# Two attention stages with the value matmuls moved ahead of one head's transposes

## The chip, the cores and the metric

The kernel runs on one core of a Trainium2 chip. The metric is the device time of one launch in microseconds (us); lower is better. TensorE is written PE, VectorE DVE, ScalarE ACT, GpSimd POOL and SyncE SP.

## The reference

Two transformer blocks follow each other on a sequence of 1024 tokens with 1024 channels, all in float32. The change touches the attention of each. The first block has neighbourhood attention with 8 heads of 64 channels: a token sees 8 rows by 16 columns of a grid of 16 by 64 tokens. The second has full attention with 8 query heads that share 2 key and value heads:

```
def attend_block(q_blk):
    scores = jnp.einsum('bqhgd,bkhd->bhgqk', q_blk, k).astype(jnp.float32) * scale
    p = jax.nn.softmax(scores, axis=-1).astype(v.dtype)
    return jnp.einsum('bhgqk,bkhd->bqhgd', p, v)
```

Around them lie the input projections, a chunked delta-rule recurrence, a Fourier mixer, output projections and two SwiGLU networks. None of those is touched.

## The kernel before

Every engine has its own program, written out as a Python loop of instructions and semaphore waits, and each engine does its program strictly in order. The phases follow each other: input projection, neighbourhood attention ("na"), delta rule, output projection, first SwiGLU, mixer, full attention ("gqa"), output projection, second SwiGLU. Both attention phases are made by the same functions (`pe_attention`, `act_attention`, `dve_attention`, `pool_attention`).

The work of an attention phase is 32 pairs. A pair is two heads (j = 0 and 1, side by side in the partitions) by 128 query tokens; pairs 8c to 8c+7 belong to the c-th couple of heads. In gqa a pair has 1024 keys. In na it has 512 keys in four of eight pairs (t = 0, 1, 6, 7) and 576 in the other four. PE's loop has n + 4 = 36 steps. In step i, as far as the pairs exist, it does:

- the scores of pair i, both heads, into two PSUM slots of two banks each (`sring`); line 820. It waits until the slots are free: in gqa until ACT has taken the exponentials of both heads of pair i - 1, in na until DVE has added the bias and found the maxima.
- the transposes of head 1 of pair i - 1, 128 keys each, up to four to a PSUM bank; line 836. They wait for that head's exponentials.
- half of the value matmuls of two pairs, i - 3 or thereabouts: `values((i - 3) // 2, (i - 3) % 2)`; line 856. Part 0, in odd steps, waits until both heads of pair i - 2 have been copied out of PSUM.
- once in four steps, from step 5 on, `spread`: four instructions at line 865 that turn the sums of four pairs into a row of factors in one PSUM bank.
- the transposes of head 0 of pair i - 1.
- in gqa, `aside(i)`: pieces of the norm and rotation of the next couple's queries, with matmuls of their own at line 2149 (steps 1, 9, 17) and line 2156 (steps 5, 13, 21). They write into `sring` too.

Transposes and `spread` take their banks from one ring of three (`tring`). A bank is free once its content has been copied: that of head 1 by DVE (line 974), that of head 0 by ACT (line 341), the `spread` bank by ACT (line 341, the scale copy). With 1024 or 576 keys a head takes two banks, with 512 keys one; below, "a" and "b" are a head's first and second bank.

ACT's step i: exponentials of pair i, head 0, then head 1 (line 918, each with a read of the accumulated sum behind it); the scale copy if there is one; the copies of head 0 of pair i - 1; its asides. DVE's step i: the maxima of pair i, head 0, then head 1 (line 968 in gqa, 963 and 346 in na); once in four steps a reciprocal; the copies of head 1 of pair i - 1; once in four steps, the product with the scales (line 993), and its asides.

Of the kernel before, what the change touches and what calls it, by code (L numbers as in the profile page):

```python
# [111 lines left out]
def build(nc, A):  # L112
# [673 lines left out]
    def value_steps(u):  # L786
        if u.nk % 128 == 0:
            return [(i, 128, 0, 256) for i in range(u.nk // 128)]
        return [(1, 128, 0, 256), (2, 128, 0, 256), (3, 128, 0, 256), (0, 128, 0, 128), (4, 64, 0, 128),
                (4, 128, 128, 256), (5, 64, 128, 256)]  # L790

    def group_at(S, i, after):

        g = (i - after - 3) // 4
        if i >= after + 3 and (i - after - 3) % 4 == 0 and g < len(S.pairs) // 4:
            return g

    def pe_attention(e, w, S, operands, aside):

        T, pairs = S.T, S.pairs
        n = len(pairs)

        def scores(u):
            (qh, ql), (kh, kl), _, ready = operands(u)
            places = [S.sring.take((u.i, j), [(S.top if S.bias else S.exp, (u.i, j))]) for j in range(2)]
            for _, before in places:
                for s, key in before:
                    w.wait_ge(s, key)  # L810
            for s, key in ready:
                w.wait_ge(s, key)
            a = tok[u.t]
            for c in u.banks:
                b = slice(c, min(u.nk, c + 512))
                k = slice(u.k0 + b.start, u.k0 + b.stop)
                for x, (q, kk) in enumerate(((qh, kh), (qh, kl), (ql, kh))):
                    for j in range(2):
                        r = rows_of(j)
                        m = e.matmul(places[j][0][:, b], q[r, a], kk[r, k], start=x == 0, stop=x == 2)  # L820
                        if x == 2 and c == u.banks[-1]:
                            m.then_inc(*S.score.up((u.i, j)))

        def turn_bank(key, until):
            p, before = S.tring.take(key, until)
            for s, key in before:
                w.wait_ge(s, key)
            return p

        def transposes(u, j):  # L830
            w.wait_ge(S.exp, (u.i, j))
            for c0 in u.banks:
                p = turn_bank((u.i, c0, j), [(S.copied[j], (u.i, c0))])
                for c in range(c0, min(u.nk, c0 + 512), 128):
                    k = min(128, u.nk - c)
                    m = e.transpose(p[0:k, c - c0:c - c0 + 128], S.P(u.i, j)[:, c:c + k], IDENT)  # L836
                m.then_inc(*S.turn.up((u.i, c0, j)))

        def values(two, part):
            u = pairs[2 * two + 1]  # L840
            _, _, V, ready = operands(u)
            steps = value_steps(u)
            if part == 0:
                if two >= 2 and two % 2 == 0:
                    w.wait_ge(S.out, two // 2 - 1)
                for s, key in ready:
                    w.wait_ge(s, key)
                for j in range(2):
                    w.wait_ge(S.copied[j], u.last)
            q0 = 256 * (two % 2)  # L850
            half = (len(steps) + 1) // 2
            for x in (range(half), range(half, len(steps)))[part]:
                kt, k, a, b = steps[x]
                v = u.base // 128 + kt
                for j in range(2):
                    m = e.matmul(S.o[rows_of(j), q0 + a:q0 + b], V[0:k, v, rows_of(j)], S.PT(u.i, j)[0:k, kt, a:b],  # L856
                                 start=x == 0, stop=x == len(steps) - 1)
            m.then_inc(*S.value.up((two, part)))

        def spread(g):  # L860

            p = turn_bank(("scale", g), [(S.scale, g)])
            w.wait_ge(S.diag, g)
            for j in range(2):
                m = e.matmul(p[rows_of(j), :], ONES[:, 0:64], T.diag[:, j, :, :].rearrange("p t n -> p (t n)"),
                             start=True, stop=True)
            m.then_inc(*S.spread.up(g))

        for i in range(n + 4):
            if i < n:  # L870
                scores(pairs[i])
            if 0 <= i - 1 < n:
                transposes(pairs[i - 1], 1)
            if 0 <= i - 3 < n:
                values((i - 3) // 2, (i - 3) % 2)
            g = group_at(S, i, 2)
            if g is not None:
                spread(g)
            if 0 <= i - 1 < n:
                transposes(pairs[i - 1], 0)  # L880
            aside(i)

# [145 lines left out]
    def pe_na(e, w):  # L1028
        pe_attention(e, w, NA, na_operands, lambda i: None)
# [1206 lines left out]
    def pe_gqa(e, w):  # L2236
        def values():
            p = gq_place(w, "v", [(v_copy, 0)])
            w.wait_ge(first_load[1], 1)
            for t in tok:  # L2240
                m = e.transpose(p[:, t], Q_.first[1][:, t], IDENT)
            m.then_inc(*v_turn.up(0))
        first_norms(e, w, pe_norm, values)
        pe_attention(e, w, GQ, gqa_operands, norms_between(e, w, pe_norm))
# [382 lines left out]
```

## Time and profile before

| | |
|---|---|
| median of the runs shown (3001.87 to 3010.09) | 3004.83 us |
| the profiled execution | 3002.75 us |
| its span in the trace | 3001.0 us |
| PE busy | 2738.3 us, 91% of the span |
| ACT, DVE, POOL busy | 37%, 40%, 40% |
| na attention on PE, first scores to last full step | 466.8 to about 582 us |
| gqa attention on PE, its end | about 2173 us |

The span runs from the first to the last instruction; the profiled execution's own time is 1.75 us longer, and is the one that compares with the runs. The maxima, exponentials and copies of both attention phases run beside PE on their own engines. A matmul's record begins when PE starts it, and its end is modelled, so the distance from one start to the next is what PE spends; a transpose's record is 0.27 us long although one starts every 0.11 us.

### The profile page before, as it was taken

The numbers are of one execution on the slowest core, as the hardware profiler recorded it, in microseconds if no ns is written. First come the engines' busy times: TensorE is split into PE (matmuls) and PEld (weight loads), VectorE is DVE, ScalarE is ACT, GpSimd is POOL, SyncE is SP. The second block draws the span as 40 slices with busy tenths as digits, with TensorE's granted clock in tenths as the row PEclk, the third lists the DMA queues.
The fourth block names the chain that finished last, engine by engine and source line by source line (L and its number), as shares of the span: only waits on it lengthen the run. The fifth ranks groups of instructions, "written<-read, shape, count | busy, mean of one in ns | idle before, by whom it ended". The sixth has DMA issues, their size and how long they took to land.

```text
span 3001.0 us, 33532 instructions
## 1 busy us (share of the span) xinstructions
PE 2738.3 (91%) x13547; PEld 2196.6 (73%) x13547; DVE 1185.7 (40%) x1729; ACT 1097.1 (37%) x1604; POOL 1187.6 (40%) x568
## 2 busy tenths in 40 slices
PE   6999987936969999999999999479999999999997
PEld 4777774536968888878888788356678888788885
DVE  6565555576574222222222421367652221222223
ACT  4444435513443422233322422256544222332222
POOL 2212112230006545556555643311165555565554
PEclk8999998968989999999999999799999999999998
DMA  3223203262034222232222232200032222233322
GB/s 125 88 95 127 91 39 121 80 227 67 24 101 146 97 99 98 92 105 99 98 99 99 97 127 78 85 8 8 2 126 98 99 98 93 98 107 104 114 98 77
DMA packets 96330, 280.05 MB, mean 93 GB/s; under 512 B 26344, under 2 KB 26536, under 8 KB 96048
## 3 DMA queue, kind: packets, MB, share of 16 engines
q1 hardware_dynamic: 96176, 277.91, 26.8%
q8 instruction: 108, 1.77, 0.2%
q14 instruction: 46, 0.38, 0.0%
HBM read 245.30 MB, written 32.57 MB: 93 GB/s over the span
## 4 chain that ended last, share of the span: by engine, by line
PE 80%; DVE 8%; ACT 4%; DMA 2%; issue 2%; POOL 2%; SPq 1%; POOLq 0%; DVEq 0%; ACTq 0%
PE ps L325 22%; PE ps L326 22%; PE ps L327 22%; ACT t L341 3%; PE ps L820 3%; PE ps L836 2%; PE ps L856 2%; PE ps L466 1%; DVE t L1288 1%; DVE t L1285 1%; DVE t L600 1%; DVE t L968 1%; POOL t L1660 1%; DVE t L963 1%; POOL t L390 0%
## 5 line engine op out<-in xcount | busy, mean ns | idle before, releaser
L341 ACT ACTIVATE t<-t 128x1024 fp32r<-128x1024 f32 (+5 forms) x981 | 751.3, 810 | 1578.1 <-PE ps L327 677.2
L390 POOL TENSOR_TENSOR t<-t 128x1024 fp32r<-128x1024 f32 x363 | 875.9, 2416 | 1001.0 <-ACT t L341 1001.0
L325 PE MATMUL ps<-t 128*128 128x512 f32 (+1 forms) x3096 | 1223.0, 395 | 50.9 <-DVE t L503 19.0
L326 PE MATMUL ps<-t 128*128 128x512 f32 (+1 forms) x3096 | 1207.1, 390 | 0.0
L327 PE MATMUL ps<-t 128*128 128x512 f32 (+1 forms) x3096 | 1206.9, 390 | 0.0
L325 PEld LDWEIGHTS ps<-t 128*128 128x128 f32 x3096 | 584.5, 189 | 191.9 <-issue 55.3
L326 PEld LDWEIGHTS ps<-t 128*128 128x128 f32 x3096 | 584.9, 189 | 122.3 <-issue 5.4
L327 PEld LDWEIGHTS ps<-t 128*128 128x128 f32 x3096 | 584.6, 189 | 121.6
L1876 DVE SCALAR_TENSOR_TENSOR t<-ps,t 128x512 f32<-128x512 f32 x192 | 132.7, 691 | 315.7 <-PE ps L327 277.2
L1932 POOL TENSOR_TENSOR t<-t 128x512 fp32r<-128x512 f32 x84 | 108.8, 1296 | 332.3 <-ACT t L341 332.3
L1853 DVE TENSOR_TENSOR t<-ps,t 128x512 f32<-128x512 f32 x84 | 58.1, 692 | 396.2 <-PE ps L327 396.2
L1847 DVE TENSOR_TENSOR t<-ps,t 128x512 f32<-128x512 f32 x88 | 60.9, 692 | 329.8 <-PE ps L327 329.7
L341 ACT ACTIVATE t<-ps 128x512 f32<-128x512 f32 (+5 forms) x230 | 116.1, 541 | 123.7 <-PE ps L1208 37.5
L820 PE MATMUL ps<-t 64*128 64x512 f32 (+1 forms) x672 | 91.9, 402 | 46.0 <-POOL t L1048 22.2
L836 PEld LDWEIGHTS ps<-t 128*128 128x128 f32 (+1 forms) x800 | 85.5, 140 | 58.8 <-issue 25.5
L836 PE MATMUL ps<-t 128*128 128x128 f32 (+1 forms) x800 | 119.1, 283 | 9.5 <-DVE t L974 9.4
L942 POOL TENSOR_TENSOR t<-t 128x1024 f32<-128x1024 f32 x16 | 30.6, 1911 | 232.7 <-DVE t L985 206.8
L820 PEld LDWEIGHTS ps<-t 64*128 64x128 f32 x672 | 61.3, 192 | 69.9 <-issue 49.1
L918 ACT ACTIVATE t<-ps,t 128x1024 f32<-128x1024 f32 x64 | 71.4, 1115 | 95.7 <-DVE t L968 95.5
L856 PE MATMUL ps<-t 128*64 128x256 f32 (+2 forms) x864 | 102.8, 372 | 1.4 <-ACT t L341 1.4
L968 DVE TENSOR_REDUCE t<-ps 128x1 f32<-128x1024 f32 x64 | 75.3, 1218 | 52.0 <-PE ps L820 52.0
L1660 POOL TENSOR_TENSOR t<-t 128x512 f32<-128x512 f32 x56 | 79.8, 1426 | 25.7 <-ACT t L341 25.7
(148 smaller groups left out, 1872.3 us busy)
## 6 DMA issues: line engine op xcount, KB each, us to landing
t<-in_wts_dram SPq DMA_DIRECT2D x363, 512.0 KB, 3.5
t<-pj SPq DMA_DIRECT2D x42, 512.0 KB, 5.6
pj<-t SPq DMA_DIRECT2D x32, 512.0 KB, 3.2
t<-in_rpb_dram SPq DMA_DIRECT2D x8, 736.0 KB, 6.3
t<-in_xT_dram SPq DMA_DIRECT2D x8, 512.0 KB, 10.9
t<-grow_d SPq DMA_DIRECT2D x8, 512.0 KB, 6.3
t<-beta_d SPq DMA_DIRECT2D x8, 512.0 KB, 6.7
t<-in_xT_dram SPq DMA_DIRECT2D x16, 256.0 KB, 3.8
```

The lines of the kernel that those rows point to most:

```text
L325: e.matmul(out, ah, bh, start=start, stop=False)
L326: e.matmul(out, ah, bl, start=False, stop=False)
L327: return e.matmul(out, al, bh, start=False, stop=stop)
L341: return e.activation(out, in_, fn, scale=scale)
L390: e.tensor_tensor(lo[:], T.raw[n % NR][:], hi[:].bitcast(F), SUB).then_inc(*w_lo.up(n))
L820: m = e.matmul(places[j][0][:, b], q[r, a], kk[r, k], start=x == 0, stop=x == 2)
L836: m = e.transpose(p[0:k, c - c0:c - c0 + 128], S.P(u.i, j)[:, c:c + k], IDENT)
L856: m = e.matmul(S.o[rows_of(j), q0 + a:q0 + b], V[0:k, v, rows_of(j)], S.PT(u.i, j)[0:k, kt, a:b], start=x == 0, stop=x == len(steps) - 1)
L968: e.tensor_reduce(nmx[:, 0:1], p, AX, MAX, negate=True).then_inc(*S.neg.up((u.i, j)))
L1660: e.tensor_tensor(acc, acc, squares, ADD).then_inc(*b_acc.up((stage, s, k)))
L1876: e.scalar_tensor_tensor(X[:, o, h], banks[P.name, s, i, o], 0.5, X[:, o, h], MUL, ADD).then_inc(*P.x_ready(s, i, o)[0].up((P.name, s, i, o)))
L1932: e.tensor_tensor(al, P.up(j), ah.bitcast(F), SUB).then_inc(*f_lo.up((P.name, j)))
```

## The change

The transposes of head 1 move from before the value matmuls to directly before those of head 0. No instruction is added or removed, and the other engines' programs stay as they are. `tring` hands out its banks in the order of PE's program, so the bank of `spread` now comes before those of head 1.

```diff
         for i in range(n + 4):
             if i < n:
                 scores(pairs[i])
-            if 0 <= i - 1 < n:
-                transposes(pairs[i - 1], 1)
             if 0 <= i - 3 < n:
                 values((i - 3) // 2, (i - 3) % 2)
             g = group_at(S, i, 2)
             if g is not None:
                 spread(g)
             if 0 <= i - 1 < n:
+                transposes(pairs[i - 1], 1)
                 transposes(pairs[i - 1], 0)
             aside(i)
```

## Rows read from the trace of the kernel before

**Rows 1.** The page, section 1: busy us, share of the span, instructions.

```profile
PE 2738.3 (91%) x13547; PEld 2196.6 (73%) x13547; DVE 1185.7 (40%) x1729; ACT 1097.1 (37%) x1604; POOL 1187.6 (40%) x568
```

**Rows 2.** Windows: length, busy us by engine, PEclk, DMA share, GB/s.

```profile
480.00:582.00 102.00, 99.70 (x793) 62.64 (x790) 67.68 (x211) 68.69 (x158) 34.50 (x16) 1.00 0.20 73
1976.00:2173.00 197.00, 181.16 (x1362) 119.80 (x1360) 129.60 (x149) 113.19 (x196) 29.46 (x14) 1.00 0.02 6
2013.00:2024.00 11.00, 7.75 (x50) 4.60 (x50) 4.78 (x5) 4.94 (x8) 0.00 (x0) 1.00 0.00 0
```

**Rows 3.** Timeline, gqa, step 16: start us, duration us, instructions, idle before.

```profile
2062.19 1.66 PE L820 MATMUL ps<-t 64*128 64x512 f32 x12
...
2063.79 1.09 PE L836 MATMUL ps<-t 128*128 128x128 f32 x8
2063.89 2.35 DVE L968 TENSOR_REDUCE t<-ps 128x1 f32<-128x1024 f32 x2 [1.97 <-PE ps L820]
...
2064.81 1.95 PE L856 MATMUL ps<-t 128*64 128x256 f32 x16
...
2066.27 1.24 DVE L974 COPY t<-ps 128x512 f32<-128x512 f32 x2
2066.28 1.12 ACT L918 ACTIVATE t<-ps,t 128x1024 f32<-128x1024 f32 x1
...
2066.69 1.09 PE L836 MATMUL ps<-t 128*128 128x128 f32 x8
2067.29 0.19 ACT L918 ACTIVATION_READ_ACCUMULATOR t<-ps,t 128x1 f32 x1
...
2067.71 0.50 PE L820 MATMUL ps<-t 64*128 64x512 f32 x2
```

**Rows 4.** Timeline, gqa, PE in step 32, which has no scores.

```profile
2163.27 2.00 PE L836 MATMUL ps<-t 128*128 128x128 f32 x16
```

**Rows 5.** Timeline, gqa, end of step 12, where DVE is late.

```profile
2039.39 1.24 DVE L974 COPY t<-ps 128x512 f32<-128x512 f32 x2
...
2040.08 0.66 PE L836 MATMUL ps<-t 128*128 128x128 f32 x4 [0.79 <-DVE t L974]
2040.41 0.19 ACT L918 ACTIVATION_READ_ACCUMULATOR t<-ps,t 128x1 f32 x1
...
2040.75 0.51 PE L820 MATMUL ps<-t 64*128 64x512 f32 x2
```

**Rows 6.** Timeline, gqa, step 17: with spread and the matmul of line 2149.

```profile
2070.33 1.95 PE L856 MATMUL ps<-t 128*64 128x256 f32 x16
...
2071.80 1.11 ACT L918 ACTIVATE t<-ps,t 128x1024 f32<-128x1024 f32 x1
...
2072.11 1.03 PE L865 MATMUL ps<-t 128*64 128x512 f32 x4
...
2073.07 1.09 PE L836 MATMUL ps<-t 128*128 128x128 f32 x8
2073.18 1.66 ACT L341 ACTIVATE t<-ps 128x512 f32<-128x512 f32 x3 [0.18 <-PE ps L865]
...
2075.93 1.96 PE L2149 MATMUL ps<-t 128*128 128x512 f32 x4 [1.77 <-ACT t L341]
```

**Rows 7.** Timeline, gqa, step 21: with spread and the matmul of line 2156.

```profile
2102.41 1.12 ACT L918 ACTIVATE t<-ps,t 128x1024 f32<-128x1024 f32 x1
...
2104.12 1.88 PE L2156 MATMUL ps<-t 128*128 128x512 f32 x4
```

**Rows 8.** Timeline, na, from step 25, which has spread.

```profile
562.26 0.97 PE L820 MATMUL ps<-t 64*128 64x512 f32 x6
...
562.62 0.58 ACT L341 ACTIVATE t<-ps 128x512 f32<-128x512 f32 x1
...
563.75 1.08 PE L856 MATMUL ps<-t 128*64 128x256 f32 x8
```

**Rows 9.** Timeline, na, PE's first scores after a long idle.

```profile
466.84 1.65 PE L820 MATMUL ps<-t 64*128 64x512 f32 x6 [22.24 <-POOL t L1048]
```

## The prediction

> **What bounds the kernel now.** I read the page first: PE is busy 91% of the span and no other engine above 40% [rows 1]. The change touches only the two attention phases, so I then took windows of them. In na PE is busy 99.70 of 102 us; in gqa 181.16 of 197 us; the granted clock is 1.00 in both, the 2.4 GHz level [rows 2]. So the change plays in about 320 us, of which PE idles some 20. Last I read the timeline step by step, since what matters is what follows what.
>
> A plain gqa step is 5.52 us from scores to scores (2062.19 to 2067.71) [rows 3]. PE has no gap in it: scores take 1.60 to the next start, head 1's transposes 1.02, values 1.88, head 0's transposes 1.02. But a second chain is nearly as long. The scores start 2062.19; DVE's maxima start 2063.89 and end 2066.24; ACT's second exponential starts 2066.28, and its read of the sum ends 2067.29 + 0.19 = 2067.48; only then is the slot free for the next scores, at 2067.71. How long PE needs from such a release is seen where PE did wait: the read ended 2040.41 + 0.19 = 2040.60 and the scores started 2040.75, so 0.15 [rows 5]. The chain alone therefore allows 2067.63: 5.44 us a step. **PE is only 0.08 us above the chain of scores, maxima and exponentials.** That is the reader's key to gqa: shortening PE's part gives 0.08 us a step at most.
>
> **What the change saves on PE.** Two things. First, two runs of eight transposes become one of sixteen. Step 32 has one: 2.00 us, against 1.02 + 1.09 = 2.11 for two separate ones [rows 3, 4]: 0.11 saved. Second, scores are followed by values in place of transposes. Before transposes PE spends more than before matmuls: values take 1.88 to the next start when transposes follow (2064.81 to 2066.69) and 1.78 when `spread` follows (2070.33 to 2072.11) [rows 3, 6]. No row has values behind scores. I take the bounds as 0.10 saved (the full difference just read) and 0.10 lost (the same size the other way, as nothing here excludes it), and choose 0.10 saved, since values and `spread` have the same stationary shape. Together 0.21 us a step, between 0.21 and 0.01.
>
> **Plain gqa steps.** Does the new order find its banks free? Count from the scores' start as 0. Values at 1.50, head 1's transposes at 1.50 + 1.88 = 3.38, their first bank ready at 3.38 + 0.66 = 4.04. DVE leaves its maxima at 2066.27, which is 4.08, so it loses nothing. Its copy takes about 0.64 to 0.68 (1.24 to 1.28 for two), to 4.74. Head 0's second bank is the one just copied (four banks a step from a ring of three); a waiting transpose started 0.05 behind such a copy (2039.39 + 0.64 = 2040.03, then 2040.08) [rows 5]. So it may start at 4.79; unhindered it would at 3.38 + 12/16 of 1.93 = 4.83. No wait, by a hair. Then 0.53 to the scores: 5.36, which is before the 5.44 that ACT allows. Result 5.44 against 5.52: **-0.08**. Of steps 3 to 31, seven have a `spread` (5, 9, ..., 29) and three (4, 12, 20) wait for a DVE that is late with norm work [rows 5] and stay as they are; 19 are plain: 19 x -0.08 = -1.5 us. If PE's reaction to ACT were the 0.05 of the other wait, it would be -0.16 each, -3.0. If values behind scores lose 0.10, PE's part is 5.36 + 0.20 = 5.56 and a step +0.04: +0.8.
>
> **Steps with spread.** Here lies the cost. Before, the order is head 1 (two banks), `spread` (third), head 0, whose first bank DVE has long copied. Now `spread` is first, head 1 takes the other two, and head 0's first bank is that of `spread`. It is free only after ACT's scale copy, and ACT does that behind both exponentials. Queued behind the waiting transpose are head 0's whole run, the aside's matmuls and the next scores; behind head 0's run wait ACT's copies of it.
>
> - Step 17 [rows 6]: the second exponential ends 2072.91; the scale copy of 0.60 (1.66 for three, overlapping) ends about 2073.50; head 0 can start 2073.55 in place of 2073.07: +0.48. ACT's copies and its Square then shift by the same, and line 2149's matmul, which already waits 1.77 for ACT, with them. Step 9 is its twin: 2 x 0.48 = +1.0.
> - Steps 25 and 29 have no aside; the same distances (exponential to scale copy to head 0) give scores 0.49 later: +1.0.
> - Step 21 [rows 7]: the exponential ends 2103.53, scale copy 2104.11, head 0 from 2104.16, line 2156's matmul 0.93 later, 2105.09 in place of 2104.12: +0.97. DVE's sine product and the next scores wait for that matmul already, so it all counts. Steps 5 and 13 are alike: +2.9.
>
> The step's own saving of 0.2 is lost in the wait. Together +4.9 for seven steps. Draining, step 32 joins its transposes as well: -0.1. gqa: -1.5 + 4.9 - 0.1 = **+3.3 us** (+1.8 with the quicker reaction).
>
> **na.** Scores wait for DVE only, and PE is almost full. But in odd steps the values wait for ACT's copies of the pair before, which head 1's transposes cover today. In step 25 that copy ends 562.62 + 0.58 = 563.20; the values start 563.75, 0.55 later, behind scores (0.90) and transposes (0.59) [rows 8]. With the transposes gone from there and the step before 0.25 shorter (0.21, and up to 0.04 more by joining runs of four), scores would start 562.01 and values be ready 562.81, but wait till 563.25, 0.44 late. From there: 0.91 values, 0.96 `spread`, 1.02 for eight transposes: scores at 566.14, against 566.21 before. So two steps win 0.07 in all; the cover is gone and eats the saving. Reading the eight steps of one couple in this way: this pair -0.07; steps 18 and 19 alike -0.07; step 23 -0.2; steps 20 and 22 wait for DVE's maxima and copy in both orders, 0; step 21 (`spread`, two banks a head) waits for the scale copy, +0.15. -0.2 a couple, four couples: **-0.8 us**. If values behind scores lose 0.10, about +0.3.
>
> **Sum.** +3.3 - 0.8 = +2.5 us, between +0.5 (quick reaction, and a little more in na) and +5.9 (values behind scores lose 0.10: 2.3 dearer in gqa, 1.1 in na). Against the profiled execution's 3002.75 that is 3005.2; that execution is 2.08 below the median of the runs shown, so as a median 3004.83 + 2.5 = 3007.3; I say **3007**. 0.3% of the time, 9 us, is about what a measurement of this kernel can tell from no change; this is a quarter of it.
>
> **Rivals.**
> 1. *PE's own time decides, and the saving is kept.* If exponentials and copies give way as PE speeds up, all 29 full steps of each phase gain 0.21: -12 us, 2993. For it: PE has no gap in a plain step [rows 3]. Against it: the 0.08 of slack in gqa, and the values' wait in na [rows 8]; both are start times of other engines, which the order on PE does not move. 4 in 100.
> 2. *The clock falls, slower.* The change lengthens idle stretches of PE in the five steps where an aside and `spread` meet (5, 9, 13, 17, 21). If there the granted clock fell to its 1.2 GHz level, the price can be read at the start of na: six scores took 1.65 us behind 22.24 us of idling, and 0.97 at full clock [rows 8, 9]. Two such groups and a run of transposes at the low level cost about 3 x 0.7 = 2.1 us; five times 10.5, with the sum above +13: 3018. Against it: step 9 with its waits, 7.75 busy of 11 us, shows 1.00 [rows 2], and it grows only by 0.5; the other three by 1.0. It decides if a single one of the five shows less than 1.00. 4 in 100. The Trainium skill ("TensorE: Matmul & The Clock Gate", Part 4: PE-mode transpose) says that transposes do not count as PE activity for the clock gate, which would make a run of sixteen beside a wait look idle; by that rule this rival would come true, and no row here shows a fall yet.
> 3. *The ring's edge gives way.* In plain gqa steps head 0's second bank is free 0.04 before it is wanted. Were DVE's copy late there as in step 12, by 0.79 [rows 5], scores would start at 4.83 + 0.79 + 0.53 = 6.15, +0.63 over 5.52; 19 steps: +12, and with the rest 3020. Against it: DVE has idled 1.97 before its maxima and has no other work in these steps. It begins to cost only when the bank is over 0.16 late. 2 in 100.
>
> **Chances and range.** The forecast has 90 in 100, with values from +0.5 to +5.9 and a scatter of the median of some 4 us: 2999 to 3014, which leaves out rival 1, rivals 2 and 3, and a little of the forecast. Faster by over 0.3% 4 in 100, within it 90, slower 6.
>
> **What would show it.** Right: plain gqa steps of 5.44 with PE waiting for ACT ahead of the scores; head 0's transposes in steps 9, 17, 25, 29 waiting for ACT (line 341), the aside matmul of step 21 later by about 1.0 in its step; in na, values in odd steps waiting for ACT. PE's busy time falls by about 10 us while the span does not. Wrong: a plain step under 5.40 or over 5.52, a granted clock under 1.00 inside gqa, or a wait of DVE's copies for PE that pushes maxima.

## The result, and the profile after

The changed kernel takes 1.0017 times the time before, with a 95% interval of 1.0010 to 1.0024: medians 3012.45 us (22 runs) against 3006.01 (22 runs). That ratio is +5.1 us of 3006, with an interval of 3.0 to 7.2 us; the two medians lie 6.4 apart. The forecast was a difference under 0.3% of the time, and +2.5 us in the sum: both the bound and the sign held, the size was half of what came.

The page of the changed kernel (its lines behind 872 have moved up by one: 917 is 918 of before, 973 is 974) answers to [rows 1]:

```profile
PE 2732.6 (91%) x13547; PEld 2195.7 (73%) x13547; DVE 1190.3 (40%) x1729; ACT 1096.0 (36%) x1604; POOL 1187.5 (39%) x568
```

PE works 5.7 us less, and the span has become longer, 3008.1 against 3001.0 us. To see where, I cut both traces at the first scores of each step. The two phases, na from step 3 and gqa from step 0, each to the first scores of step 31, in the windows view (length, busy us by engine, clock); first the changed kernel:

```profile
478.35:588.91 110.56, 104.84 (x850) 68.68 (x850) 74.27 (x228) 73.50 (x172) 34.44 (x16) 1.00 0.19 71
1950.23:2164.92 214.69, 184.48 (x1352) 122.59 (x1352) 139.05 (x154) 119.78 (x205) 27.53 (x13) 0.98 0.02 6
```

and the kernel before:

```profile
476.82:586.27 109.45, 107.11 (x851) 67.58 (x852) 72.78 (x228) 73.99 (x172) 34.50 (x16) 1.00 0.19 72
1948.05:2158.78 210.73, 185.35 (x1353) 123.08 (x1354) 137.01 (x154) 120.18 (x205) 27.55 (x13) 0.98 0.02 6
```

na has grown by 1.11 us and gqa by 3.96, +5.07 in all. That this is so close to the +5.1 of the runs is partly chance, as the interval above is 4 us wide and one trace is one execution. The clock of 0.98 in both gqa rows comes from steps 0 and 1 alone (0.75 and 0.86 in both kernels); every later step shows 1.00. The other 2 us between the two spans lie ahead of na (1.1), in its first three steps (0.4), between the phases (-0.5) and behind (1.0); the last experiment shows how much such stretches vary. Step by step (us from one step's first scores to the next's):

```
gqa                   before   after  difference x count
plain steps (18)        5.52    5.50   -0.3 together
4, 12, 20               6.61    6.61    0.0
25, 29                  6.38    6.86   +0.48 x 2
9, 17                  11.65   11.97   +0.32 x 2
5                      10.51   11.38   +0.87
13, 21                 10.41   11.29   +0.88 x 2
na (steps modulo 8)
2 and 3                 7.29    7.35   +0.06
4                       4.09    4.09    0.0
5 (spread)              5.06    5.34   +0.28
6                       3.62    3.67   +0.05
7                       3.73    3.58   -0.15
0 and 1 (spread)        7.12    7.06   -0.06
```

A plain gqa step of the changed kernel, timeline, answering to [rows 3]:

```profile
2066.31 1.67 PE L820 MATMUL ps<-t 64*128 64x512 f32 x12
2067.91 1.95 PE L856 MATMUL ps<-t 128*64 128x256 f32 x16
...
2069.79 2.10 PE L836 MATMUL ps<-t 128*128 128x128 f32 x16
...
2070.49 1.29 DVE L973 COPY t<-ps 128x512 f32<-128x512 f32 x2
...
2071.42 0.19 ACT L917 ACTIVATION_READ_ACCUMULATOR t<-ps,t 128x1 f32 x1
...
2071.82 0.50 PE L820 MATMUL ps<-t 64*128 64x512 f32 x2
```

The reader is to see three numbers. Values start 1.60 behind the scores, as the transposes did (2063.79 - 2062.19) [rows 3]: nothing is saved there. The run of sixteen takes 2.10, not the 2.00 of [rows 4]: it stands 0.10 for its last bank, whose copy by DVE starts 2070.49, takes 0.69 and ends 2071.18. And the next scores start 0.21 behind the end of ACT's read (2071.42 + 0.19 = 2071.61), where a real wait for it is 0.15 [rows 5]: PE does not wait for ACT here. In the 18 plain steps of this trace that distance is 0.20 to 0.23.

Step 25, with `spread`, and the middle of step 21:

```profile
2132.57 1.03 PE L865 MATMUL ps<-t 128*64 128x512 f32 x4
...
2133.28 1.12 ACT L917 ACTIVATE t<-ps,t 128x1024 f32<-128x1024 f32 x1
2133.53 1.09 PE L836 MATMUL ps<-t 128*128 128x128 f32 x8
...
2134.39 0.59 ACT L341 ACTIVATE t<-ps 128x512 f32<-128x512 f32 x1
2135.03 1.09 PE L836 MATMUL ps<-t 128*128 128x128 f32 x8 [0.41 <-ACT t L341]
```

```profile
2107.92 0.59 ACT L341 ACTIVATE t<-ps 128x512 f32<-128x512 f32 x1
2108.56 1.09 PE L836 MATMUL ps<-t 128*128 128x128 f32 x8 [1.75 <-ACT t L341]
```

Head 0's transposes start 0.05 behind the end of ACT's scale copy (2134.98 and 2108.51). `spread` itself had long ended: ACT was at its exponentials. Among PE's waits in gqa (waiting line, whom for, us, times, longest) the largest in total is one that the kernel before does not have:

```profile
PE ps L836 <- ACT t L341: 7.0, 7, 1.8
```

### The profile page after: what moved, and what is told of

Same layout as the page of the kernel before. It is cut to its first block, busy times and chain, and to the rows that moved or that the text cites. A ratio compares the mean times of both kernels' runs of the same rounds, so it can differ in the third digit from the quotient of the medians.

```text
span 3008.1 us, 33507 instructions
## 1 busy us (share of the span) xinstructions
PE 2732.6 (91%) x13547; PEld 2195.7 (73%) x13547; DVE 1190.3 (40%) x1729; ACT 1096.0 (36%) x1604; POOL 1187.5 (39%) x568
## 3 DMA queue, kind: packets, MB, share of 16 engines
q8 instruction: 108, 1.77, 0.2%
## 4 chain that ended last, share of the span: by engine, by line
PE 78%; DVE 8%; ACT 5%; issue 3%; DMA 2%; POOL 2%; SPq 0%; POOLq 0%; DVEq 0%; ACTq 0%
PE ps L325 22%; PE ps L327 22%; PE ps L326 22%; ACT t L341 3%; PE ps L820 2%; PE ps L836 2%; PE ps L856 2%; ACT t L917 1%; PE ps L466 1%; DVE t L962 1%; DVE t L967 1%; DVE t L600 1%; POOL t L1659 1%; POOL t L390 0%; PE ps L1170 0%
## 5 line engine op out<-in xcount | busy, mean ns | idle before, releaser
L836 PE MATMUL ps<-t 128*128 128x128 f32 (+1 forms) x800 | 111.5, 281 | 16.9 <-DVE t L973 9.6
```

## The experiments

My theory: the cost lies in seven gqa steps and four na steps with two banks a head, where head 0's first bank is that of `spread` and ACT empties it behind both exponentials; and in na's values, which wait for ACT's copies. The main rival: values ahead of both heads' transposes, or the run of sixteen, is dear in itself. Ratios are to the kernel before, measured beside each.

**1. Spread between the two heads.** On the changed kernel:

```diff
                 values((i - 3) // 2, (i - 3) % 2)
+            if 0 <= i - 1 < n:
+                transposes(pairs[i - 1], 1)
             g = group_at(S, i, 2)
             if g is not None:
                 spread(g)
             if 0 <= i - 1 < n:
-                transposes(pairs[i - 1], 1)
                 transposes(pairs[i - 1], 0)
```

> Order: scores, values, head 1's transposes, spread, head 0's transposes; so values stay ahead of the transposes, but spread no longer takes the bank that head 0 needs. My theory (the cost is head 0's wait for the scale copy, plus values waiting for ACT's copies in the neighbourhood attention): in the full attention steps 25 and 29 return from 6.86 to about 6.38 us, steps 5, 13, 21 from 11.3 to 10.4, steps 9 and 17 from 11.97 to 11.65, plain steps stay 5.50; the full attention from its first to its last scores takes 210.4 us (before 210.7, after 214.7). Neighbourhood attention: steps 5, 13, 21, 29 return from 5.34 to 5.06, steps 9, 17, 25 are dearer, 4.1 to 4.3; in all 120.5 us (before 119.4, after 121.0). Time about 0.8 us above before, same. Rival (running values ahead of both heads' transposes is itself the cost, wherever spread stands): steps 25 and 29 stay near 6.8, and the time stays 5 us above before.

Measured: gqa 211.0 us; steps 13 and 21 10.41, steps 9 and 17 11.80, 25 and 29 6.54, plain 5.50. na's steps 5 and 1 modulo 8, which have `spread`, 5.21 and 4.33, na 110.9 from step 3. So gqa gives back 3.7 of its 3.96 us, as the theory has it; 0.16 stays in steps 25 and 29 and 0.15 in 9 and 17, which it did not have. In na step 5 gave back only half of its 0.28, where 5.06 was expected; step 1 grew by 0.3, about as expected (4.1 to 4.3). The ratio, 1.0013 (1.0004 to 1.0021), is above the +1.8 us that the two phases show, but its interval reaches it.

**2. Only the bank order changed.** On the kernel before, `spread` moves ahead of head 1's transposes, and values stay between the heads:

```diff
                 scores(pairs[i])
+            g = group_at(S, i, 2)
+            if g is not None:
+                spread(g)
             if 0 <= i - 1 < n:
                 transposes(pairs[i - 1], 1)
             if 0 <= i - 3 < n:
                 values((i - 3) // 2, (i - 3) % 2)
-            g = group_at(S, i, 2)
-            if g is not None:
-                spread(g)
```

> Order: scores, spread, head 1's transposes, values, head 0's transposes: the old order, but spread takes its bank ahead of head 1, as in the changed kernel. My theory (the order of banks alone makes the cost): full attention steps 25 and 29 take 6.86 as in the changed kernel (before 6.38), steps 5, 13, 21 take 11.3 (before 10.4), plain steps 5.52; 215 us in all against 210.7. In the neighbourhood attention spread now comes before POOL has made its input, so 0.5 to 1 us more in each of eight steps, which says nothing on the theory. Rival (the cost comes from the transposes standing in one run behind the values): the full attention stays at 210.7.

Measured in one execution: steps 25 and 29 6.86 and 6.85, 5, 13, 21 11.38, 11.29, 11.29, 9 and 17 11.98; plain 5.52; gqa 215.06. Every number of the changed kernel's dear steps without any run of sixteen. Step 25:

```profile
2135.72 1.95 PE L856 MATMUL ps<-t 128*64 128x256 f32 x16
...
2136.18 1.11 ACT L918 ACTIVATE t<-ps,t 128x1024 f32<-128x1024 f32 x1
...
2137.29 0.59 ACT L341 ACTIVATE t<-ps 128x512 f32<-128x512 f32 x1
2137.93 1.09 PE L836 MATMUL ps<-t 128*128 128x128 f32 x8 [0.26 <-ACT t L341]
```

This decides against the rival. na took 114.0 us from step 3: its steps 1 modulo 8 grew by 1.1 us each, since `spread` now came ahead of POOL's product (in step 9, PE idles 0.88 before `spread` until POOL's line 942 ends).

**3. Head 0 first.** On the changed kernel, the last two lines swap:

```diff
             if 0 <= i - 1 < n:
-                transposes(pairs[i - 1], 1)
                 transposes(pairs[i - 1], 0)
+                transposes(pairs[i - 1], 1)
```

> Order: scores, values, spread, head 0's transposes, then head 1's. Now the fourth bank of a step is the one that ACT empties, and ACT copies only behind both exponentials. My theory (who empties the fourth bank sets the step): plain full attention steps take 6.38 us in place of 5.50 (exponential ends 5.21 after the scores' start, copy 0.59, start 0.05, four transposes 0.53), steps 4, 12, 20 about 7.5, the whole full attention about 234 us; neighbourhood attention about 10 us more; time about 3040. Rival (PE's own time sets the step and the ring has room): the plain steps stay within 0.05 of 5.50 and the time with them.

Measured in one execution: 3047.91 us, 8 more than expected; plain steps 6.47 to 6.49, gqa 241.3, na 119.7 from step 3. The timeline of step 22: twelve transposes, then the last four wait for ACT.

```profile
2143.26 1.53 PE L836 MATMUL ps<-t 128*128 128x128 f32 x12
...
2143.93 1.11 ACT L918 ACTIVATE t<-ps,t 128x1024 f32<-128x1024 f32 x1
...
2145.04 1.07 ACT L341 ACTIVATE t<-ps 128x512 f32<-128x512 f32 x2
2145.68 0.66 PE L836 MATMUL ps<-t 128*128 128x128 f32 x4 [0.89 <-ACT t L341]
```

The mechanism is the expected one, and costs one microsecond a step. The estimate for gqa was 7 us short: steps 4, 12 and 20 (6.75) cost less than expected, but steps 1, 2, 3, 5 and 21 up to 2.8 us more (13.67, 8.21, 7.87, 13.17, 13.14), and in these the granted clock was low, 0.67 over steps 0 and 1, 0.71 over 2, 0.66 over 3, 0.87 over 5 and over 21; step 13, with 1.00, took 11.54.

**4. The change in gqa alone.** In na the old order stays:

```diff
-            if 0 <= i - 1 < n:
+            if S.bias and 0 <= i - 1 < n:
                 transposes(pairs[i - 1], 1)
...
+            if not S.bias and 0 <= i - 1 < n:
+                transposes(pairs[i - 1], 1)
```

> The changed order in the full attention alone; the neighbourhood attention as before. My theory: neighbourhood attention 119.4 us from first to last scores as before, full attention 214.7 as in the changed kernel, so 4 us of the 5.5 that the two traces show; time about 4 us above before, within 0.3%. Rival (the two phases' costs are not separate, the later one inherits a delay of the earlier): full attention differs from 214.7 by over 0.5 us.

Measured: 1.0016 (1.0007 to 1.0025). na from step 3 109.46 us, as before. gqa 216.08, the steps from 2 on are those of the changed kernel but for one: step 17 took 13.51, 1.54 more. There the granted clock fell:

```profile
2080.00:2082.00 2.00, 2.00 (x3) 0.97 (x4) 0.00 (x0) 0.00 (x0) 0.00 (x0) 0.50 0.00 0
```

Without it gqa is 214.5, as the theory has it. That opened rival 2 of the prediction again: was the fall the change's doing? Experiment 9 answers.

**5. The new order only where nothing waits.** On the kernel before, `new` steps have values ahead of head 1:

```diff
+            g = group_at(S, i, 2)
+            new = g is None and not (S.bias and i % 8 == 3)
-            if 0 <= i - 1 < n:
+            if not new and 0 <= i - 1 < n:
                 transposes(pairs[i - 1], 1)
...
+            if new and 0 <= i - 1 < n:
+                transposes(pairs[i - 1], 1)
```

> The new order only in steps without spread, and in the neighbourhood attention not in steps 3, 11, 19, 27 either (there the values would wait for ACT's copies). My theory (all of the cost sits in the steps left out here): full attention 210.2 us from first to last scores (before 210.7, changed kernel 214.7), neighbourhood attention 107.6 us from step 3 to step 31 against 109.45 before and 110.56 in the changed kernel: steps 2, 7, 8 modulo 8 each 0.14 shorter and the odd steps behind them not longer. Time about 2 us below before, which is within 0.3% and hardly to be told. Rival (values ahead of both heads' transposes cost something in every step): the two phases are no shorter than before.

Measured: na 108.33 us from step 3 (before 109.45): steps 2, 7, 0 modulo 8 at 3.20, 3.58, 3.02 and step 3 back at 3.96, so -1.1, where -1.8 was hoped. gqa 211.68, of which 1.37 is a clock fall in step 9 (13.02, clock 0.87 over the step); without it 210.3. The steps did what the theory says. The time did not follow: the ratio 1.0009 (1.0000 to 1.0018) is +2.7 us, where the two phases give -1.5 without the clock fall and -0.2 with it. This trace has its extra time ahead of na and between the phases, where the programs are alike; the cause stays open.

**6. The rotation ahead of head 0.** The traces show the matmul of line 2156, DVE's sine product and the next scores standing behind head 0's transposes. On the kernel before:

```diff
+            first = not S.bias and i in (5, 13, 21)
+            if first:
+                aside(i)
             if 0 <= i - 1 < n:
                 transposes(pairs[i - 1], 0)
-            aside(i)
+            if not first:
+                aside(i)
```

> The kernel before, with the aside of steps 5, 13, 21 of the full attention (PE's rotation matmul) ahead of head 0's transposes in place of behind them. The traces say that the rotation, DVE's sine product and the next scores form a chain that waits for head 0's transposes in both kernels, and by 0.9 us more in the changed one. If so, these steps take about 8.9 us in place of 10.4 and the full attention 206.1 in place of 210.7; time 4 to 5 us below before. Rival (the chain is held by ACT's or DVE's own work): the three steps stay within 0.2 of 10.4.

Measured: steps 5, 13, 21 at 9.03, 8.94, 8.94, gqa 206.36 us; 0.9991 (0.9982 to 0.9999). The steps are as expected; the time fell by 2.7 us, where 4 to 5 was expected.

**7. Both edits.** Experiments 5 and 6 together.

> The two edits before together. By my theory they add: full attention 205.6 us, neighbourhood attention as in the kernel with chosen steps, time 6 to 7 us below before (0.2%), faster than both kernels. Rival (the edits share one slack, so the second gives nothing): the time is that of the better single edit.

Measured: gqa 205.83, na 108.34 from step 3: they add. 0.9990 (0.9982 to 0.9999), a median of 3001.25 us (11 runs) against 3004.57 (27 runs): faster than both kernels, but by 3 us, half of what was expected. (That it beats the changed kernel follows from the two ratios to the kernel before; they were not measured side by side.) Step 21, timeline: head 0's transposes now lie beside DVE's product.

```profile
2099.95 1.98 PE L2163 MATMUL ps<-t 128*128 128x512 f32 x4
...
2101.77 1.04 PE L836 MATMUL ps<-t 128*128 128x128 f32 x8
2101.97 1.23 DVE L2208 TENSOR_TENSOR t<-ps,t 128x1024 f32<-128x1024 f32 x1 [0.99 <-PE ps L2163]
...
2103.34 0.97 PE L820 MATMUL ps<-t 64*128 64x512 f32 x6 [0.53 <-DVE t L2208]
```

**8. DVE makes the scale copy.** On the changed kernel; only the engine that empties the bank differs (the semaphore goes over to DVE with it):

```diff
 # dve_attention, ahead of the copies of pair i - 1; taken out of act_attention
+            g = group_at(S, i, 2)
+            if g is not None:
+                w.wait_ge(S.spread, g)
+                if g:
+                    w.wait_ge(S.out, g - 1)
+                e.tensor_copy(T.scale[:], S.tring["scale", g]).then_inc(*S.scale.up(g))
```

> The changed order, but the scale copy is done by DVE ahead of its copies of head 1, in place of ACT behind both exponentials. The work is the same; only who empties the bank that head 0 needs is changed. My theory (head 0 waits for ACT's place in the queue, not for its own order): full attention steps 25 and 29 fall from 6.86 to about 6.4, steps 5, 13, 21 from 11.3 to about 10.5, steps 9 and 17 from 11.97 to about 11.65, full attention 214.7 to about 211; neighbourhood steps 5, 13, 21, 29 from 5.34 to about 5.1. Time 3 to 4 us below the changed kernel. Rival (the run of sixteen transposes is slow of itself in these steps): the steps stay as in the changed kernel.

Measured: steps 25 and 29 6.38, 5, 13, 21 10.51, 10.41, 10.41, step 17 11.60: the dear steps of gqa are gone with PE's order unchanged. Step 25:

```profile
2129.31 1.03 PE L865 MATMUL ps<-t 128*64 128x512 f32 x4
...
2130.27 2.12 PE L836 MATMUL ps<-t 128*128 128x128 f32 x16
2130.39 0.69 DVE L984 COPY t<-ps 128x512 f32<-128x512 f32 x1 [0.39 <-PE ps L865]
```

Sixteen transposes in one run again, 2.12 us. gqa as a whole was 211.84, with a clock fall in step 9 (13.16). In na the step stayed at 5.36 to 5.39: the expected 5.1 was wrong, as there head 0's second bank waits for DVE, which now has one copy more ahead of it. Ratio 1.0006 (0.9998 to 1.0015), against 1.0017 of the changed kernel: 3.3 us lower, as expected, though the intervals overlap.

In the six experiments with a ratio (1, 4, 5, 6, 7, 8) it lies 1 to 4 us above what the two phases give without clock falls. Each but two (5 and 7) agrees with its steps within its interval, but all lie on one side. Clock falls that are more frequent than in the kernel before would do that; no run here counts them, and it stays open.

**9. Both kernels once more.** Unaltered, one execution each, for a second trace.

> The changed kernel unaltered, for a second trace. Asked: do the step times repeat (5.50, 6.86, 11.3, 11.97 in the full attention), and does the granted clock fall in step 9 or 17 of the full attention, as it did once in each of two other kernels? My theory expects the same steps within 0.05 and, should a clock fall come, about 1.4 us for it. Rival: the steps with spread differ from run to run by as much as the change made them differ.

> The kernel before unaltered, for a second trace. Asked: how much do the stages that the change does not touch, and the first three steps of the neighbourhood attention, differ between executions of one program? My theory: the first steps take 3.48 and up to 3.5 us in some runs of this kernel too (before showed 3.30 and 3.09 once), and the untouched stages differ by 1 to 2 us, so that only the step times tell a change of this size apart. Rival: they repeat within 0.3 us, and then what the changed kernel showed there belongs to the change.

Measured: the steps repeat. The changed kernel again has na 110.56 us from step 3, steps 13 and 21 11.29, 25 and 29 6.85 and 6.86; the kernel before again 109.47, 10.41, 10.42, 6.38, 6.38. But the clock falls in the kernel before as well, in step 9 and in step 17 of one execution; the windows of the two steps, and of 2 us in the first:

```profile
2013.36:2026.54 13.18, 9.94 (x53) 5.09 (x53) 4.77 (x5) 5.70 (x10) 0.63 (x1) 0.87 0.00 0
...
2022.00:2024.00 2.00, 2.00 (x3) 0.66 (x2) 0.00 (x0) 0.00 (x0) 0.00 (x0) 0.50 0.00 0
2071.15:2084.09 12.94, 9.69 (x53) 5.08 (x53) 4.77 (x5) 5.69 (x10) 0.63 (x1) 0.87 0.00 0
```

```profile
2021.58 3.49 PE L2149 MATMUL ps<-t 128*128 128x512 f32 x4 [1.77 <-ACT t L341]
```

The four matmuls of line 2149 take 3.49 us, against 1.96 at full clock [rows 6], after the same 1.77 of idle. The untouched stages differ too: between the phases 1362.36 here against 1361.78; in the changed kernel 1355.06 against 1361.32, far more than the expected 1 to 2 us; behind gqa 828.96 against 827.51; na's first three steps 10.64 against 9.98, in the same program. The rival of the second expectation is out: what the changed kernel showed in na's first steps needs no change to come about.

## Why the prediction was right, and its size half

- **PE is barely above the chain of scores, maxima and exponentials.** The plain steps kept their length, but not for this reason. The chain sets a floor of 5.44, and the step came out at 5.50: PE never waited for ACT's exponential there (the scores start 0.20 to 0.23 behind its read, not 0.15), so the floor itself was not put to the test. By the rows, what held the step was the ring, "no wait, by a hair" (no experiment takes that wait away alone). Joining the runs saved about 0.10, and the wait for DVE's copy took 0.10 back; values behind scores cost what transposes cost (1.60), inside my bounds. The prediction wanted the thirteenth transpose 12/16 of 1.93 = 1.45 behind the first. In [rows 4] it starts 1.37 behind (2164.64, in the row below), so the bank was wanted 0.08 earlier than counted. And DVE's copy starts when head 1's first four transposes are done (4.17 behind the scores, not 4.08) and takes 0.69, not 0.66. Eighteen steps gave -0.3, and step 31 with the draining steps nothing, in place of -1.6 for all. The same slip is in the sum: 5.52 less the 0.21 saved is 5.31, not 5.36. With 5.31 the bad case would be 5.51 a step in place of 5.56, and the upper end about +4.9 in place of +5.9.

The kernel before, timeline from 2164.91: the run of [rows 4] from its thirteenth transpose on.

```profile
2164.64 0.63 PE L836 MATMUL ps<-t 128*128 128x128 f32 x4
```

- **Steps with spread.** Right in place, cause and order of size: experiments 2 and 8 show it, one by making the cost without the run, one by removing it and keeping the run. +4.2 in place of +4.9: 0.48 in steps 25 and 29 as forecast, 0.88 in place of 0.97 in 5, 13, 21, and 0.32 in place of 0.48 in 9 and 17. In step 21 the matmul of line 2156 came 0.97 later in its step (2109.49, 8.09 behind the step's first scores, against 7.12), just as forecast. The 0.09 that is missing lies in the hand-over from DVE's sine product to the scores, 0.05 in place of the 0.15 of before; in steps 9 and 17 two such hand-overs took 0.05.
- **na.** The sign was wrong, and the forecast's own bounds (-0.8 to about +0.3) did not hold it: +1.1 came. The values do wait for ACT's copies (steps 3, 11, 19, 27, 0.26 idle before line 856 in step 19), and experiment 5 shows it: with the old order in these steps they are back at 3.96. The pair read in detail, steps 24 and 25, came as forecast (-0.06 for -0.07). The pairs taken to be alike did not: steps 18 and 19 gave +0.06. Behind scores nothing was saved, and values started 0.15, not 0.05, behind ACT's copy. Step 5 modulo 8 cost 0.28 in place of 0.15, as its last bank waits for DVE's copy as well. Step 3, without a partner before it, I had left out: +0.19.
- **The sum.** The forecast's four terms, -1.5, +4.9, -0.1 and -0.8, came as -0.3, +4.2, 0.0 and +1.1. The sign rests on the spread steps, which were understood. That the total still fell below +5.9 was luck in part: that end stood for dearer values behind scores, which did not come. PE's busy time fell by 5.7 us, where about 10 was expected.
- **Rival 1** (PE's saving is kept) fell. **Rival 2** (the clock falls by the change) did not decide: from step 2 on, the changed kernel's first trace has no fall, its second has one in step 9 (13.52) and one in step 2 (6.67 in place of 5.40); the kernel before has none in its first and two in its second, at the same price. The mechanism exists, 1.3 to 1.6 us a fall in place of the 2.1 I priced. It came with the old order of step 9 too (experiment 5), and stayed away in experiment 2, whose steps 9 and 17 wait as in the changed kernel; whether the change makes falls more frequent, so few traces cannot tell. So the sign "a granted clock under 1.00 inside gqa" did come, but does not speak against the forecast, as the kernel before shows it as well. The Trainium skill ("TensorE: Matmul & The Clock Gate", Part 4: PE-mode transpose) says that transposes do not count as PE activity in the way that other matmuls do. The 18 plain steps with a run of sixteen show 1.00 in each trace of the changed kernel, so such a run alone, among other matmuls, did not lower the clock; more on the rule these runs cannot tell. **Rival 3** (the ring's edge) came true in kind: the bank was late in every plain step, by 0.10 and not by 0.79, and took what PE had saved; experiment 3 shows what it costs when it goes wide.

## What to carry to other kernels

When matmul groups share a ring of PSUM banks, write down for each group whose bank it takes over, which engine empties it, and what stands ahead of that copy in the engine's queue; an order on PE changes all three. A gap-free PE is not yet the bound: measure each loop through the other engines, that of the banks too, and count only what is above the longest (here the loop through ACT left 0.08 a step, and the ring took most of that). And where four takes go round three banks, a margin of a few hundredths of a microsecond in a forecast is no margin.

## What the runs showed of the hardware

- The granted clock halved to 0.50 for about the length of four matmuls in steps 9 and 17 of gqa, behind a run of eight or sixteen transposes (sixteen in experiment 8) and 1.7 to 1.8 us of idling, in some executions and not in others of one program: in both steps in the second trace of the kernel before, in neither in its first. Experiment 3, with the most idling on PE in gqa (45.5 of 241.3 us), had the most of it. Each fall from full clock costs 1.3 to 1.6 us.
- A transpose group costs more at its edges than inside: two runs of eight take 2.11 us and one of sixteen 2.00 [rows 3, 4]; what follows scores, be it transposes, values or `spread` (in experiment 2, 2132.10 to 2133.69), starts 1.59 or 1.60 behind them.
- PE starts 0.05 us behind some hand-overs and 0.15 behind others, even at one line: line 2149 started 0.15 behind ACT's Square in the kernel before, and 0.05 in the changed one. What sets which, no run here was made to tell.
